# Branch output and memory transposed by quarters, their two parts made straight from PSUM

## The reference

```
n = rms_norm(h, g_mix);  proj = n @ w_in
gates = sigmoid(proj[..., SPLIT_V:])
y_ssd = ssd_mixer(z, xbc, dt, ...) @ w_ssd_out        # ends in rms_norm(y, g_ssd), per group of 512
y_sb  = stick_breaking_attention(q, k, v) @ w_sb_out
h = h + (gates[..., :D] * y_ssd + gates[..., D:] * y_sb) @ w_out
h = h + memory_cross_attention(rms_norm(h, g_xattn), rms_norm(mem, g_mem), w_xq, w_xkv, w_xo)
h = h + moe_ffn(rms_norm(h, g_moe), ...)              # top 4 of 32 experts, 12 MB of f32 weights each
out = rms_norm(h, g_final)
```

## Time and profile before

| | |
|---|---|
| median of 3 runs | 1315.87 us (1315.59 to 1319.79) |
| the profiled execution, its own time | 1318.25 us |
| its span (first to last instruction) | 1316.4 us |
| PE busy | 1221.2 us, 93% |
| DVE, ACT, POOL busy | 311.3, 230.5, 230.8 us |
| DMA | 452.03 MB, mean 343 GB/s |
| mean granted clock of PE | 0.972 of full |

### The profile page before, as it was taken

How to read it: one execution, slowest core, us unless ns; L and a number is a source line. 1 busy time by engine, 2 the same in 40 slices (tenths; PEclk the granted TensorE clock), 3 DMA queues, 4 the chain that set the end, 5 groups by cost and what they waited for, 6 DMA issues and landing times.

```text
span 1316.4 us, 13854 instructions
## 1 busy us (share of the span) xinstructions
PE 1221.2 (93%) x5869; PEld 603.4 (46%) x5869; DVE 311.3 (24%) x452; ACT 230.5 (18%) x284; POOL 230.8 (18%) x205
## 2 busy tenths in 40 slices
PE   5999997898799999999999999999999999999996
PEld 5987776787643333333333333333333333333332
DVE  3526354314231112122111111211111111111111
ACT  4463674245100000000000000100000000000001
POOL 6776746776000000000000000000000000000000
PEclk9999998899879999999999999999999999999999
DMA  9543423454719999999999999999999999999994
GB/s 296 186 140 123 160 96 108 160 176 183 328 61 418 428 429 426 427 428 427 428 428 426 429 428 428 426 427 428 429 428 427 427 429 428 427 427 428 427 427 184
DMA packets 51498, 452.03 MB, mean 343 GB/s; under 512 B 4060, under 2 KB 4216, under 8 KB 26696
## 3 DMA queue, kind: packets, MB, share of 16 engines
q1 hardware_dynamic: 50680, 448.85, 82.8%
q0 software_dynamic: 752, 2.21, 0.6%
HBM read 450.00 MB, written 1.05 MB: 343 GB/s over the span
## 4 chain that ended last, share of the span: by engine, by line
PE 69%; DMA 24%; DVE 2%; issue 2%; ACT 1%; POOL 0%; POOLq 0%; SPq 0%; ACTq 0%; DVEq 0%
PE ps L920 23%; DMA ring<-in_w_gu 13%; PE ps L962 12%; PE ps L605 11%; DMA gates_xn<-in_w_gu 10%; PE ps L592 7%; PE ps L859 4%; PE ps L885 3%; PE ps L893 3%; PE ps L620 1%; PE ps L943 1%; PE ps L935 1%; PE ps L755 0%; PE ps L697 0%; DMA h<-in_x 0%
## 5 line engine op out<-in xcount | busy, mean ns | idle before, releaser
L385 POOL TENSOR_TENSOR w_parts<-ring,w_parts 128x512 fp32r<-128x512 f32 x160 | 214.1, 1371 | 84.8 <-ACT w_parts L1013 84.6
L920 PE MATMUL ps<-ring,nT 128*64 128x512 f32 x768 | 175.2, 604 | 17.8 <-DMA ring<-in_w_gu 17.8
L920 PE MATMUL ps<-ring,xs 128*64 128x512 f32 x768 | 175.1, 608 | 9.6 <-DMA ring<-in_w_gu 5.2
L480 POOL TENSOR_SCALAR ss<-ss 128x2 f32<-128x2 f32 (+2 forms) x7 | 1.3, 191 | 995.0 <-ACT junk L1003 975.0
L962 PE MATMUL ps<-ring,xbuf 128*64 128x512 f32 x768 | 171.4, 595 | 0.7 <-issue 0.7
L1209 ACT ACTIVATE xbuf<-xbuf 128x512 f32<-128x512 f32 x32 | 20.1, 630 | 780.1 <-DVE xbuf L1622 780.1
L1622 DVE TENSOR_SCALAR xbuf<-ps 128x512 f32<-128x512 f32 x32 | 22.1, 692 | 454.9 <-PE ps L920 454.9
L605 PE MATMUL ps<-w_parts,xT_hi 128*128 128x512 f32 x352 | 113.7, 404 | 8.9 <-issue 8.9
L920 PEld LDWEIGHTS ps<-ring,nT 128*64 128x64 f32 x768 | 54.3, 139 | 135.6 <-issue 101.6
L920 PEld LDWEIGHTS ps<-ring,xs 128*64 128x64 f32 x768 | 55.6, 140 | 125.7 <-issue 112.9
L962 PEld LDWEIGHTS ps<-ring,xbuf 128*64 128x64 f32 x768 | 53.4, 137 | 115.1 <-issue 115.1
(11 more groups left out here) (276 smaller groups left out, 1098.8 us busy)
## 6 DMA issues: line engine op xcount, KB each, us to landing
ring<-in_w_gu SPq DMA_DIRECT2D x96, 2048.0 KB, 30.1
ring<-in_w_down SPq DMA_DIRECT2D x47, 2048.0 KB, 35.1
kv_small<-in_w_gu SPq DMA_DIRECT2D x16, 2048.0 KB, 29.9
gates_xn<-in_w_gu SPq DMA_DIRECT2D x16, 2048.0 KB, 31.2
ring<-in_w_in SPq DMA_DIRECT2D x24, 1024.0 KB, 5.2
gates_xn<-in_w_down SPq DMA_DIRECT2D x8, 2048.0 KB, 35.2
kv_small<-in_w_down SPq DMA_DIRECT2D x8, 2048.0 KB, 33.4
ring<-in_w_ssd_out SPq DMA_DIRECT2D x4, 1024.0 KB, 5.0
```

The lines of the kernel that those rows point to most:

```text
L385: ops.tensor_tensor(w_lo[:, m % SPLIT, c], ring_slot(m)[:, c], w_hi[:, m % SPLIT, c], ALU.subtract).then_inc(lo_ready[name], 1)
L920: i = mm(ps[64 * half:64 * half + 64, 4 + q, :], xg[:, k, (j % GE) * SLOTS:(j % GE + 1) * SLOTS], w[:, q * FF + half * 512:q * FF + half * ...
```

## The change

For y and the memory the transposed copy in SBUF is gone. PE transposes by quarters (`pair_transposes`): quarter j is two k tiles of 256 tokens in one bank, `K_BANK[j]`. ACT makes hi of each tile from PSUM with the gain as scale (`high_tiles`), and DVE makes lo from PSUM in one instruction, PSUM times gain minus hi (`low_tiles`). PE waits tile by tile (`tiles=`), on semaphores of their own: `y_hi`, `y_lo`, `m_hi`, `m_lo`. The first half of y is transposed between the two chunks of the last gate stripe, the second after it. The memory is transposed after the first `ssd_out` stripe. `mem_hi` moves from `scr` to `kv`, and the pair `kv_small` waits in addition for the last `xv` chunk.

```diff
+K_BANK = (5, 7, 4, 6)
-        mem_hi = nc.alloc_sbuf_tensor_at("mem_hi", [P, KD, T], F32R, offset=aligned_of["scr"])
+        mem_hi = nc.alloc_sbuf_tensor_at("mem_hi", [P, KD, T], F32R, offset=kv_at)
@@ sync, first_free
                 elif PAIR_ORDER[q] == KV_SMALL:
                     sp_.wait_ge(normed, NORMED[TR_MERGED])
                     sp_.wait_ge(xa_lg, H_XA)
+                    sp_.wait_ge(chunk_used, products_done(FIRST["xv"]))
@@ tensor, channel_products and token_products alike
                         if b == 0:
+                            if tiles is not None:
+                                pe.wait_ge(tiles, 4 * c + k + 1)
                             low_tile(CHUNK_AT[(n, c)], k)
@@ tensor
+            def pair_transposes(src, quarters):
+
+                for j in quarters:
+                    for k in (2 * j, 2 * j + 1):
+                        for b in range(TB):
+                            i = nc.tensor.transpose(ps[:, K_BANK[j], k % 2 * T + b * P:k % 2 * T + (b + 1) * P],
+                                                    src[:, b, k * P:(k + 1) * P], ident[:])
+                    i.then_inc(tr_done, 1)
@@ tensor
             sb_values(2)
             sb_values(3)
+            pe.wait_ge(normed, NORMED[TR_Y])
+            pe.wait_ge(sb_min, 4)
+            pair_transposes(xs, (0, 1))
             stripe(FIRST["gate"] + 3, xT, parts=(1,))
             pe.wait_ge(sb_out, 4)
-            transposes(TR_Y, xs)
-            for n in range(2):
-                stripe(FIRST["ssd_out"] + 2 * n, xT, tr=TR_Y)
-                stripe(FIRST["sb_out"] + 2 * n, sbT2)
-            transposes(TR_MEM, memx)
-            stripe(FIRST["xk"], memT2, parts=(0,), tr=TR_MEM)
-            pe.wait_ge(tr_out, 4 * TR_MEM + 4)
+            pair_transposes(xs, (2, 3))
+            stripe(FIRST["ssd_out"], xT, tiles=y_lo)
+            pe.wait_ge(y_lo, KD)
+            pe.wait_ge(normed, NORMED[TR_MEM])
+            pair_transposes(memx, (0, 1, 2, 3))
+            stripe(FIRST["sb_out"], sbT2)
+            stripe(FIRST["ssd_out"] + 2, xT)
+            stripe(FIRST["sb_out"] + 2, sbT2)
+            stripe(FIRST["xk"], memT2, parts=(0,), tiles=m_lo)
+            pe.wait_ge(m_lo, KD)
             transposes(TR_MERGED, merged)
-            stripe(FIRST["xk"], memT2, parts=(1,), tr=TR_MEM)
+            stripe(FIRST["xk"], memT2, parts=(1,), tiles=m_lo)
@@ scalar
+            def high_tiles(tr, hi, gain, quarters, ready):
+
+                for j in quarters:
+                    act.wait_ge(tr_done, 4 * tr + j + 1)
+                    for k in (2 * j, 2 * j + 1):
+                        af(hi[:, k, :], ps[:, K_BANK[j], k % 2 * T:(k % 2 + 1) * T], ACT.Copy,
+                           scale=gain[:, k:k + 1]).then_inc(ready, 1)
@@ scalar
+            splits_to(CHUNK_AT[(FIRST["ssd_out"], 1)])
+            high_tiles(TR_Y, xT_hi, pcol[:, ROW_SSD:ROW_SSD + KD], (0, 1), y_hi)
+            high_tiles(TR_Y, xT_hi, pcol[:, ROW_SSD:ROW_SSD + KD], (2, 3), y_hi)
             empty(FIRST["gate"] + 3)
-            high_parts(TR_Y, xT_hi, nT)
...
-            splits_to(31)
-            high_parts(TR_MEM, mem_hi, memT)
+            splits_to(28)
+            high_tiles(TR_MEM, mem_hi, pcol[:, ROW_MEM:ROW_MEM + KD], (0, 1, 2, 3), m_hi)
             splits_to(32)
@@ vector
+            def low_tiles(lo, hi, gain, quarters, high, ready):
+
+                for j in quarters:
+                    dve.wait_ge(high, 2 * j + 2)
+                    for k in (2 * j, 2 * j + 1):
+                        V.scalar_tensor_tensor(out=lo[:, k, :], in0=ps[:, K_BANK[j], k % 2 * T:(k % 2 + 1) * T],
+                                               scalar=gain[:, k:k + 1], in1=hi[:, k, :], op0=ALU.mult,
+                                               op1=ALU.subtract).then_inc(ready, 1)
+
+            g_ssd_k = pcol[:, ROW_SSD:ROW_SSD + KD]
+            low_tiles(xT_lo, xT_hi, g_ssd_k, (0, 1), y_hi, y_lo)
             dve.wait_ge(rstd, 3)
             normalise(memx, memx, 2, blocks=(0, 1))
-            take_transposed(TR_Y, nT, pcol[:, ROW_SSD:ROW_SSD + KD])
-            low_parts(TR_Y, xT_lo, nT, xT_hi)
+            low_tiles(xT_lo, xT_hi, g_ssd_k, (2, 3), y_hi, y_lo)
...
                 dve.wait_ge(normed, NORMED[TR_MEM] + n + 1)
-            take_transposed(TR_MEM, memT, pcol[:, ROW_MEM:ROW_MEM + KD])
-            low_parts(TR_MEM, mem_lo, memT, mem_hi)
+                if n == 0:
+                    low_tiles(mem_lo, mem_hi, pcol[:, ROW_MEM:ROW_MEM + KD], (0, 1, 2, 3), m_hi, m_lo)
```

More of the change, by code:

```diff
@@ L156 @@
 NORMED = [1, 3, 5, 7, 8, 9]
-XLO = {TR_X: (1, 2), TR_Y: (3, 4), TR_MEM: (5, 6), TR_MERGED: (8, 10), TR_H1: (11, 12)}
-TAKEN = {TR_X: 0, TR_Y: 4, TR_MEM: 8, TR_H1: 12, TR_H2: 16}
+XLO = {TR_X: (1, 2), TR_MERGED: (4, 6), TR_H1: (7, 8)}
+TAKEN = {TR_X: 0, TR_H1: 4, TR_H2: 8}
+K_BANK = (5, 7, 4, 6)
 SQUARED = {"x": 1, "y": 5, "mem": 7, "h1": 8, "h2": 9, "final0": 10, "final1": 11}
@@ L280, in build @@
         dtT = scr[0:H_SSD, 2, 0:T]
-        memT = xs[:].rearrange("p b d -> p (b d)").rearrange("p (k t) -> p k t", t=T)
         gfac = scr2
@@ L344, in build @@
         tr_done, tr_out = sem("tr_done"), sem("tr_out")
+        y_hi, y_lo, m_hi, m_lo = sem("y_hi"), sem("y_lo"), sem("m_hi"), sem("m_lo")
         pt_done, pcol_ready = sem("pt_done"), sem("pcol_ready")
@@ L553, in _, with stripe @@
             xT, memT2, sbT2, oT2 = (xT_hi, xT_lo), (mem_hi, mem_lo), (sb_hi, sb_lo), (o_hi, o_lo)
-            def stripe(n, src, parts=(0, 1), tr=None):
+            def stripe(n, src, parts=(0, 1), tr=None, tiles=None):
                 _, _, _, kt, layout, _ = STRIPES[n]
@@ L568, in stripe @@
                     if layout == "channel":
-                        channel_products(n, src, c, b0)
+                        channel_products(n, src, c, b0, tiles)
                     else:
-                        token_products(n, src, c, b0)
+                        token_products(n, src, c, b0, tiles)
             def low_tile(m, k):
@@ L581, in pairs, with channel_products @@
                 return [(hi, src[0]), (lo, src[0]), (hi, src[1])]
-            def channel_products(n, src, c, b0):
+            def channel_products(n, src, c, b0, tiles):
                 passes = pairs(CHUNK_AT[(n, c)], src)
@@ L596, in channel_products, with token_products @@
                 i.then_inc(chunk_used, 1)
-            def token_products(n, src, c, b0):
+            def token_products(n, src, c, b0, tiles):
                 passes = pairs(CHUNK_AT[(n, c)], src)
@@ L836, in _ @@
             transposes(TR_H2, hn2)
-            pe.wait_ge(tr_out, 20)
+            pe.wait_ge(tr_out, 12)
             pe.wait_ge(late_in, 48)
@@ L1481, in _ @@
                 dve.wait_ge(normed, NORMED[TR_MEM] + n + 1)
-            take_transposed(TR_MEM, memT, pcol[:, ROW_MEM:ROW_MEM + KD])
-            low_parts(TR_MEM, mem_lo, memT, mem_hi)
+                if n == 0:
+                    low_tiles(mem_lo, mem_hi, pcol[:, ROW_MEM:ROW_MEM + KD], (0, 1, 2, 3), m_hi, m_lo)
             for half in range(2):
                 for b in range(TB):
-                    dve.wait_ge(xhi_ready, XLO[TR_MEM][1] + 2 * half + b + 1)
+                    dve.wait_ge(xhi_ready, XLO[TR_X][1] + 2 * half + b + 1)
                     k, t = slice(4 * half, 4 * half + 4), slice(b * P, (b + 1) * P)
```

## The result

Four runs each, in turns: before 1315.76 us (1315.59 to 1319.79), changed 1299.53 us (1299.28 to 1304.85). The ratio is 0.9871, with a 95% interval of 0.9847 to 0.9896: about 16 us less, faster by more than the 0.3% that can be told apart, 1.5 us above the forecast of 1298.0 and inside its range. The changed kernel was timed twice more, beside experiments: 1299.54 against 1320.48, ratio 0.9852 (0.9824 to 0.9879), and 1300.21 against 1318.31, ratio 0.9874 (0.9848 to 0.9900). The changed kernel's three medians lie within 0.7 us; those of the kernel before, 1315.76, 1318.43, 1320.48 and 1318.31 us in four series, do not, so the gain is 16 to 21 us by the series that one takes.

A forecast was written before the change was run, and what follows sets the result against it. The experts were taken as bound by their weight stream, its end set by when PE reaches the first expert. Idle 8.85 and 4.88 plus clock 2.4 and 1.8 give 17.9 us: 1315.87 - 17.9 = 1298.0 us, range 1294.5 to 1304.

The forecast's parts named there:

- Where it is bound: Experts are bound by their weight stream; each us PE gains ahead of the first expert reaches the end one for one.
- Idle time at y, 8.85 us, and at the memory, 4.88 us: PE's idle time between the transposes and the first products at y and the memory would go, 8.85 and 4.88 us.
- The tiles: ACT's hi and DVE's lo tiles from PSUM would take 0.48 us each.
- The upper bound of 1.64 us: DVE's lo tile if it contends with POOL: 1.64 us, costing a wait of 1 us at chunk 25.
- The weight chain: ACT's splits and POOL's lo for chunks 24 to 29 would be ready before PE starts each; least room 2 us, at 27.
- rival B: ACT late with the lo of chunks 27 and 28, PE waits 2 to 4 us: 1301 to 1305 us; chance 9%.
- The slow tails, 2.4 and 1.8 us: Products at a lower PE clock behind the idle at y and the memory; 2.4 and 1.8 us would be regained.
- Rival A: Transposes count as rest, so PE's clock stays lower behind them: price 4.2 us, 1302.2 us; chance 6%.
- Rival C: In SP's queue the wait of kv_small holds the loads behind it: slower, above 1319 us; chance 2%.
- Rival D: PE's "issue" wait hides another cause, such as a chunk's weights; the idle stays, 1315.9 us; chance 3%.

The follow-up runs named there:

- y alone: Changed kernel with the memory's transposes and chain put back as in the kernel before, only y by quarters from PSUM: 1305.95 us, ratio 0.9910 to the kernel before.
- the old places: Changed kernel's parts straight from PSUM, but every block of transposes where the kernel before had it: 1305.14 us, ratio 0.9904 to the kernel before.
- held POOL: Kernel before with one more wait: POOL starts chunk 26's low parts only after DVE has made y's: 1314.0 us, ratio 0.9959 to the kernel before.
- the wait alone: Kernel before with only the added wait of the pair kv_small for the last xv chunk: 1319.22 us, ratio 1.0001.
- the order alone: Changed kernel with the memory's transposes in their new place but its old gain copy, high parts and subtraction: 1298.4 us, ratio 0.9859 to the kernel before.
- chunk 38 split first: Changed kernel with h1 also by quarters from PSUM, ACT splitting chunk 38 ahead of h1's normalisation and tiles: 1298.66 us, ratio 0.9857 to the kernel before.

## Why the prediction was right

**Where it is bound.** Right. The first expert starts 18.94 us earlier in the profiles, the end of the span 18.8; y alone, the old places and the held POOL moved both together too.

**Idle time at y, 8.85 us, and at the memory, 4.88 us.** Right, all of both. The start of chunk 24 was laid out at 205.9 us and came at 205.18 (chunk 23 took 5.50 us, and the transposes 1.02 and 0.88, but `sb_values(3)` had ended 0.48 us sooner, which is most of the 0.7). What filled y's wait was read rightly from the earlier trace rows, DVE standing against POOL: held POOL showed it by taking the one thing away, and with it 5.3 of the 8.85 us; the other 3.5 are the long chain itself.

**The tiles.** Both sizes taken as 0.48 us, measured by form (mean ns of one behind the bar):

```profile
L1501 DVE SCALAR_TENSOR_TENSOR xT_lo<-ps,pcol,xT_hi 128x256 fp32r<-128x256 f32 x8 | 3.3, 478 | 2.8 <-ACT xT_hi L1078 2.8
L1501 DVE SCALAR_TENSOR_TENSOR mem_lo<-ps,pcol,mem_hi 128x256 fp32r<-128x256 f32 x8 | 3.2, 477 | 0.0
L1078 ACT ACTIVATE xT_hi<-ps,pcol 128x256 fp32r<-128x256 f32 x8 | 3.1, 476 | 5.0 <-PE ps L636 5.0
L1078 ACT ACTIVATE mem_hi<-ps,pcol 128x256 fp32r<-128x256 f32 x8 | 3.0, 485 | 0.0
```

The upper bound of 1.64 us, DVE against POOL, did not come. The prediction priced it in part wrongly: it let DVE end y's last four tiles at 212.5 us, which leaves out that at 1.64 us the first four tiles and the memory's normalisation would come later too; from about 200.4 us on, four tiles, 3.23 us of normalisation and four more tiles end at about 216.7, an estimate. As PE takes the tiles one by one, the wait stays near the 1 us it gave. The first four low tiles stand at 199.52 to 201.18 us, the memory's eight at 226.21 to 229.44, and POOL works through both (`w_parts` from 196.19 for 11.01 us, and from 216.29 on). The rule of the Trainium skill that the prediction weighed (SBUF — State Buffer, Who interferes with whom) said so for an instruction with one SBUF input, and this trace agrees: 0.48 us.

**The weight chain.** Right. ACT (start us, us, what):

```profile
209.33 1.28 ACT L1194 ACT_TABLE_LOAD   x1
210.63 3.72 ACT L1194 ACTIVATE gates<-gates 128x2048 f32<-128x2048 f32 x2
214.25 1.90 ACT L1035 ACTIVATE w_parts<-ring 128x2048 fp32r<-128x2048 f32 x1
216.40 1.92 ACT L1035 ACTIVATE w_parts<-ring 128x2048 fp32r<-128x2048 f32 x1 [0.25 <-PE ps L612]
218.22 3.01 ACT L1078 ACTIVATE mem_hi<-ps,pcol 128x256 fp32r<-128x256 f32 x8
```

Laid out: sigmoids done at 215.5, splits at 217.4 and 219.3, tiles at 223.2. Measured: 214.3, 216.2, 218.3 and 221.2. The room at chunk 27 was there, so **rival B** (9%) is refuted: PE waits at none of the chunks 24 to 31.

**The slow tails, 2.4 and 1.8 us.** Right in the profiled execution, too large for the first medians; these are the terms that were mis-sized. y alone measured 2.40 us for the first. For the second, `xk` to chunk 32 took 15.15 us before and takes 13.26: 1.89. But they were read from one execution, and the second one of the same kernel had 1.7 and 1.6 us by the same subtraction. From that one to the changed profile the span falls by 1314.4 - 1297.6 = 16.8 us, near the 16.2 of the first medians; from the first profile it falls by 18.8. The prediction subtracted tails of an execution 2.38 us above the median from the median itself. Its 17.9 us lies between both; the later series gave 20.9 and 18.1. Of the 1.7 us between 17.9 and 16.2 the smaller tails explain 0.9, the rest lies within the spread of the runs. That 1298.0 came within 1.5 us is therefore partly luck of the series: 17.9 off the second series' 1320.48 would be 1302.6, and 1299.54 was measured.

**Rival A** (6%), the clock does not come back: refuted by the windows of 1.00 over three blocks of transposes. **Rival C** (2%), the queue: refuted, no cost of the wait alone can be told (1.0001), and in the changed kernel the pair leaves at 309.34 us, is used at 372.81, and the stream still stands at rest before the first expert. **Rival D** (3%), another cause behind "issue": refuted, since the wait went where nothing but the chain was changed (0.18 us at y, tiles in the old places).

**What the prediction did not separate.** It charged both waits to chain and place together. The experiments part them in large part. At y the form of the chain, in the old order, does it, and the new order adds 0.45 us by stages; the old chain in the new order was not run there, so what the order would do alone is not shown. Nor are the two sides of the form parted, reading PSUM and letting PE go on tile by tile. At the memory the form alone takes away 3.07 of the 4.88 us; the order alone takes away all of it, and beside the order the form adds nothing.

**Left open.** Why slow stretches fall where they do, from one execution to the next. Whether the version with chunk 38 split first is faster than the change: 4.8 us less ahead of the experts in one profile, 2.5 in the other, at best 1.5 at the end.

## What to carry to other kernels

When PE waits on a short chain of other engines, look at what runs beside it before moving anything: a subtraction of two SBUF tensors took 6.54 us beside GpSimd's work and 1.2 alone, and reading one operand straight from PSUM, in tiles that the first product can use one by one, took away both that and a copy (8.85 us of idle fell to 0.18). Where independent products are at hand, placing the transposes ahead of them hides even the long chain. Price an idle stretch of PE with the slow products behind it, but take that tail from more than one execution.

## What was not expected of the hardware

The subtraction of two SBUF tensors of 128x1024 took 1.2 us alone, 2.2 us as the mean of two beside POOL, and 6.54 us when it met four tiles of POOL's: it ended 1.1 us after them (214.68 against 208.65 + 4.94 = 213.59 us, as the earlier trace rows have it), which looks more like waiting them out than like a share of speed; no run here parts the two.

An idle time of 1.81 us at the memory (tiles in the old places) left the granted clock of the following window at 1.00, from 242 to 248 us; one of 3.5 us (POOL held) was followed by 0.66, the 8.85 us by 0.51.

The runs of the kernel before lie up to 10 us apart (1314.85 to 1324.91), and profiles of equal code differ by stretches at a lower granted clock in places that no edit touches: with chunk 38 split first, `sb_values(3)` ended at 199.59 us in one profile and at 197.29 in the other.
